# Second block's pooled products on 64 rows of the array each, alternating between two PSUM tiles

## The chip, the core and the metric

The kernel runs on one core of one Trainium2 chip. The metric is the device time of one execution in microseconds. TensorE multiplies, VectorE and ScalarE do elementwise work, SyncE's queue (SP) loads the weights. A matmul of TensorE takes its weights from SBUF by a load of its own and writes its sums into PSUM; the array has 128 rows, one for each partition over which a product is summed.

## What is computed

A program of four layers on 512 tokens of width 1024: two layers of a first block, then two of a second block. In each layer of the second block, one projection gives attention operands, a short convolution's operands, a pooling operand and three gates. The change is in the pooling branch:

```python
def pooling_mixer(u, w_grp, scale):
    # u: (B, S, 256); w_grp: (4, 64, 256)
    cs = jnp.cumsum(u, axis=1)
    for g, w in enumerate((2, 4, 8, 16)):
        csg = cs[:, :, 64 * g:64 * g + 64]
        lagged = jnp.pad(csg[:, :S - w], ((0, 0), (w, 0), (0, 0)))
        groups.append((csg - lagged) / counts - u[:, :, 64 * g:64 * g + 64])
    d = jnp.stack(groups, axis=2)
    out = jnp.einsum('bsgc,gcd->bsgd', d, w_grp).reshape(B, S, 1024)
    return out * scale

merged = g[:, :, 0] * y_attn + g[:, :, 1] * y_conv + g[:, :, 2] * y_pool
x = x + merged @ w_o[l]
```

Each of the four groups has 64 channels, so its product sums over 64 values and gives 256 output channels for each of the 512 tokens.

## The kernel before

Activations lie with channels on partitions and tokens along the free axis. Every product is made of three passes of rounded operands (`wH` by `hH`, `wH` by `hL`, `wL` by `hH`: high and low parts of weights and activations), each a matmul of 128 weights by 512 tokens.

Weights arrive in **units** of 128 x 2048. SP loads a unit into one of two `raw` buffers. ScalarE rounds it into `wH` (`split`, L1255), VectorE subtracts to get `wL` (`split`, L1688), and TensorE's `take_unit` waits for `wl_ready`, which that subtraction raises. `wH` and `wL` have two buffers, so ScalarE can round a unit only when TensorE has ended the unit before the previous one.

Results go through **jobs**. The PSUM tile `G` has four banks in two halves; `take_job` waits until the reader of the job before the last has freed its half (`job_free`), `end_job` raises `job_done` on the job's last matmul. VectorE's `step` waits for `job_done`, reads the half, frees it, and then, if told so, does the next unit's `split`. `psS` and `psT` are two further PSUM tiles of two banks, used by the attention before.

The order around the change, in each of the two layers: TensorE does the last two units of the pooling gate (`plain(h_op)`), then the pooled products, then the four gate units of the convolution. The first of these is called U+1 below, the second U+2. The pooled unit holds the weights of groups 0 and 2 on partitions 0 to 63 and of groups 1 and 3 on partitions 64 to 127; so do `PX_` and `PL`, the high and low parts of the pooled operand (`pd_op`, in the tile `wsr`). For each group there are two output tiles of 128 channels, `t` = 0 and 1, with three passes each: 24 matmuls per layer. The columns of a group's weights are zero in the other group's rows (the host writes only half of the rows), and each matmul runs over all 128 rows. Group 0 goes to a half of `G`, group 1 to `psS`, group 2 to `psT`, group 3 to the other half of `G`.

VectorE's program there is written out by hand: the last pooling gate is read (`scaled`, L1811), then `pools(0)` multiplies group 0 by its scale and gate (L2635, two instructions) and, as it is a `step`, splits U+1 (L1688); then `pools(1)` and `pools(2)` read `psS` and `psT` after `pooled_done`, and `pools(3)` is again a step, which splits U+2:

```python
step(lambda g: pools(0)(g).then_inc(job_free, 1))
for jj, bank in ((1, psS), (2, psT)):
    dve.wait_ge(pooled_done, (c.lay.v - 4) * 2 + jj)
    pools(jj)(bank)
step(lambda g: pools(3)(g).then_inc(job_free, 1))
```

Other lines that the prediction's steps touch: L1134, the attention scores, which are plain fp32 matmuls over 64 rows with the two heads of a pair in different halves of the rows; L949, scores of the first block over 128 rows; L552 transposes.

Of the kernel before, what the change touches and what calls it, by code (L numbers as in the profile page):

```python
# [22 lines left out]
P = 128  # L23
S = 512
M = 256
D = 1024
KT = D // P
# [102 lines left out]
class Pos:  # L130
# [5 lines left out]
    @property  # L136
    def v(self):
        return self.base + self.off
# [73 lines left out]
def program(nc, a, out, scratch):  # L212
    ctx = contextlib.ExitStack()
    with ctx:
# [8 lines left out]
        def sb(name, shape, dt=F32):  # L223
            return ctx.enter_context(nc.sbuf_tensor(name, shape, dt))

        def sem(name):
            return ctx.enter_context(nc.semaphore(name))
# [5 lines left out]
        wH = sb("wH", [P, 2, UNIT], F32R)  # L233
        wL = sb("wL", [P, 2, UNIT], F32R)
# [32 lines left out]
        G = ctx.enter_context(nc.psum_tensor("G", [P, 4, S], F32))  # L267
        psS = ctx.enter_context(nc.psum_tensor("psS", [P, 2, S], F32))
        psT = ctx.enter_context(nc.psum_tensor("psT", [P, 2, S], F32))
# [21 lines left out]
        def blocks(t, half):  # L291

            v = t.rearrange("p (n two l) -> p n two l", two=2, l=half)
            return v[:, :, 0, :], v[:, :, 1, :]
# [7 lines left out]
        for half in (8, 16, 32, 64, 128):  # L302
            n = S // half
# [61 lines left out]
        pooled_done = sem("pooled_done")  # L365
# [74 lines left out]
        def _(pe):  # L440
            c = Counts(pe)
# [5 lines left out]
            def take_job():  # L447

                pe.wait_ge(job_free, c.job.v + 1)

            def end_job(mm):
                mm.then_inc(job_done, 1)
                c.job.off += 1

            def passes(o, w0, w1, op, k, cols, first, last, swap=False, u=None):

                u = c.unit.p if u is None else u
                for n, (w, h) in enumerate(((wH, op[0]), (wH, op[1]), (wL, op[0]))):
                    wt, mv = w[:, u, w0:w1], h[:, k, cols]
                    mm = pe.matmul(o, mv if swap else wt, wt if swap else mv,  # L460
                                   start=first and n == 0, stop=last and n == 2)
                return mm
# [206 lines left out]
            pd_op = (wsr[:, PX_:PX_ + 2, :], wsr[:, PL:PL + 2, :])  # L669
# [45 lines left out]
            for l in range(2):  # L715
                if l == 0:
# [62 lines left out]
                    for n in range(2):  # L779
                        take_unit()  # L780
                        take_job()
                        for tt in range(ST):
                            for k in range(KT):
                                mm = passes(G[:, c.job.p * 2 + tt // 2, (tt % 2) * 256:(tt % 2) * 256 + 256],
                                            k * 256, k * 256 + 256, h_op, k, slice(tt * P, tt * P + P),
                                            k == 0, k == KT - 1, swap=True)
# [6 lines left out]
                    for lev in range(8):  # L793
                        for h in range(4):
                            n = lev * 4 + h
# [16 lines left out]
                            for o, ks, qs, w in parts:  # L812
                                q = q_[:, qs:qs + w]
                                if 0 < lev < 6:
                                    o, w, q = o // 2, w // 2, blocks(q, 2 ** (lev + 1))[1]
                                mm = pe.matmul(psS[:, n % 2, o:o + w], k_[:, ks:ks + P], q, start=True, stop=True)  # L816
                            mm.then_inc(hs_done, 1)

                            if h % 2 == 1:
                                k = n // 2 % KT  # L820
# [3 lines left out]
                                for t in range(2):  # L824
                                    w0 = k * 256 + t * P
                                    mm = passes(G[:, c.job.p * 2 + t, :], w0, w0 + P, h_op, k, slice(0, S),
                                                k == 0, k == KT - 1)
# [5 lines left out]
                    for h in range(4):  # L833
                        if h % 2 == 0:
                            take_job()
                        o = G[:, c.job.p * 2 + h % 2, :]
                        v = lambda tt: ws[:, GI + tt, h * P:h * P + P]

                        for ct in range(4):
                            pe.matmul(o[:, ct * P:ct * P + P], v(ct), ws[:, DD + h, ct * P:ct * P + P],  # L840
                                      start=(ct == 0), stop=False, skip_group_check=True)
                        for m in range(2):
                            pe.matmul(o[:, 256 * m + P:256 * m + 256], v(2 * m), hsx1[:, h, m, :],
                                      start=False, stop=False, skip_group_check=True)
                        for m in range(2):
                            mm = pe.matmul(o[:, 256:512], v(m), ws[:, SX2 + h, m * 256:m * 256 + 256],
                                           start=False, stop=(m == 1), skip_group_check=True)
# [32 lines left out]
                else:  # L880
# [73 lines left out]
                    for s_ in range(32 + PV_LAG):  # L954
# [6 lines left out]
                        if 0 <= r < 32:  # L961
# [3 lines left out]
                            for kt in range(r % ST + 1):  # L965
                                mm = pe.transpose(psT[:, r % 2, kt * P:kt * P + P],
                                                  ws[:, OP + r % 4, kt * P:kt * P + P], ident[:])
                            mm.then_inc(t_done, 1)
                        r = s_ - PV_LAG
                        if r >= 0:  # L970
                            h, qt = r // ST, r % ST
# [6 lines left out]
                            for kt in range(qt + 1):  # L978
                                mm = pe.matmul(G[:, 1 + 2 * (h % 2), qt * P:qt * P + P], ov[:, kt, h * P:h * P + P],
                                               opt[:, h % 2, kt, qt * P:qt * P + P], start=(kt == 0), stop=(kt == qt))  # L980
# [69 lines left out]
            for l in c.layers(2, **LAYER):  # L1050
# [5 lines left out]
                for k in range(KT):  # L1056
                    for n, (w, h) in enumerate(((fH, hH), (fH, hL), (fL, hH))):
                        mm = pe.matmul(G[:, c.job.p * 2, :], w[:, k * 8:k * 8 + P], h[:, k, :],  # L1058
                                       start=(k == 0 and n == 0), stop=(k == KT - 1 and n == 2))
# [3 lines left out]
                def token(tt, o):  # L1063
                    for k in range(KT):
                        mm = passes(o, k * 256, k * 256 + 256, h_op, k, slice(tt * P, tt * P + P),
                                    k == 0, k == KT - 1, swap=True)
                    return mm
# [3 lines left out]
                for tt in range(ST):  # L1071
                    mm = token(tt, G[:, c.job.p * 2 + tt // 2, (tt % 2) * 256:(tt % 2) * 256 + 256])
# [65 lines left out]
                def pv_pair(r):  # L1138
                    qt = fox_row(r)[1]
                    for kt in range(qt + 1):  # L1140
                        for h in (fox_row(r)[0], fox_row(r + 1)[0]):
                            lo = 64 * (h % 2)
                            mm = pe.matmul(G[lo:lo + 64, (h // 2) % 2 * 2 + 1, qt * P:qt * P + P],  # L1143
                                           ws[:, FV + kt, h * 64:h * 64 + 64], fpt[:, h % 2, kt, qt * P:qt * P + P],
                                           start=(kt == 0), stop=(kt == qt))
                    return mm
# [5 lines left out]
                for d in range(16 + 2):  # L1152
# [12 lines left out]
                    if 1 <= d <= 16:  # L1165
                        for r in (2 * d - 2, 2 * d - 1):
                            pe.wait_ge(p_ready, c.row.v + (r + 1))
                            wait(pe, pt_ready, c.row.v + (r - 1))
                            for kt in range(fox_row(r)[1] + 1):
                                mm = pe.transpose(psT[:, r % 2, kt * P:kt * P + P],  # L1170
                                                  ws[:, FP + r % 4, kt * P:kt * P + P], ident[:])
# [5 lines left out]
                    if r >= 0:  # L1177
# [9 lines left out]
                        mm = pv_pair(r)  # L1187
# [10 lines left out]

                take_unit()
                pe.wait_ge(pdl_ready, c.lay.v - 3)  # L1200
                for jj, bank in enumerate((None, psS, psT, None)):
                    if bank is None:
                        take_job()
                    for t in range(2):
                        o = 2 * jj + t
                        dst = G[:, c.job.p * 2 + t, :] if bank is None else bank[:, t, :]
                        mm = passes(dst, (KT + o) * P, (KT + o + 1) * P, pd_op, o // 4, slice(0, S), True, True)
                    if bank is None:
                        end_job(mm)
                    else:  # L1210
                        mm.then_inc(pooled_done, 1)
                c.unit.off += 1

                for n in range(4):
# [1659 lines left out]
```

## Time and profile before

| | us |
|---|---|
| three runs, median (lowest to highest) | 3120.57 (3120.07 to 3120.65) |
| span of the profiled execution | 3119.4 |
| TensorE busy with matmuls | 3097.3 (99%) |
| VectorE busy | 1563.7 (50%) |
| ScalarE busy | 1063.2 (34%) |
| TensorE's share of the chain that ended last | 91% |

The span runs from the first to the last instruction of one profiled execution; a run's time holds some 1.2 us more. "Busy" of TensorE counts a matmul from its issue to its end, and matmuls are pipelined, so starts are what to compare. The chain that ended last is followed back from the last instruction, at each step to what released it.

### The profile page before, as it was taken

How to read it: one execution, taken by the hardware profiler on the slowest of the kernel's cores; microseconds unless marked ns; L12 is line 12 of the kernel's file. 1: busy time of each engine (PE TensorE's matmuls, PEld its weight loads, DVE VectorE, ACT ScalarE, POOL GpSimd, SP SyncE). 2: the span in 40 equal slices, each digit the busy share in tenths (PEclk: the TensorE clock that was granted, in tenths of full speed). 3: DMA queues.
4: the chain of work that ended last, by engine and by line, in shares of the span. 5: the costliest groups of instructions: out<-in, count | busy, mean ns of one | idle time of the engine just before them, and what ended most of it. 6: DMA issues, size and time to landing. Idle time of an engine off the chain costs nothing.

```text
span 3119.4 us, 37101 instructions
## 1 busy us (share of the span) xinstructions
PE 3097.3 (99%) x15540; PEld 2594.3 (83%) x15540; DVE 1563.7 (50%) x1889; ACT 1063.2 (34%) x1155; POOL 237.6 (8%) x139
## 2 busy tenths in 40 slices
PE   9999999999999999999999999999999999999999
PEld 7798988888889798888888778888888878888887
DVE  7564555554335554555435764544433766444432
ACT  3223343443223433444323332333323332333321
POOL 0002100010000020010000000111000000100100
PEclk9999999999999999999999999999999999999999
DMA  4412412223321131222233122222232322222222
GB/s 170 115 55 73 144 55 90 99 94 108 120 97 68 48 142 55 85 99 99 95 108 116 58 92 101 90 99 93 103 108 89 95 82 95 95 95 96 94 106 95
DMA packets 47567, 297.72 MB, mean 95 GB/s; under 512 B 7075, under 2 KB 7331, under 8 KB 13396
## 3 DMA queue, kind: packets, MB, share of 16 engines
q1 hardware_dynamic: 42336, 285.91, 25.9%
q10 hardware_dynamic: 5108, 10.02, 1.4%
q8 instruction: 96, 1.57, 0.2%
q14 instruction: 27, 0.22, 0.0%
HBM read 291.16 MB, written 4.75 MB: 95 GB/s over the span
## 4 chain that ended last, share of the span: by engine, by line
PE 91%; DVE 5%; ACT 2%; issue 1%; DMA 0%; ACTq 0%; POOL 0%; DVEq 0%; SPq 0%
PE G L460 83%; DVE wL L1688 1%; ACT wH L1255 1%; PE psS L816 1%; DVE mxt L1920 1%; PE psS L520 1%; PE psS L1017 1%; PE psS L1134 0%; PE G L1143 0%; PE G L1024 0%; PE psT L552 0%; DVE ws L2477 0%; PE psT L1170 0%; PE G L1058 0%; PE psS L949 0%
## 5 line engine op out<-in xcount | busy, mean ns | idle before, releaser
L460 PE MATMUL G<-hH,wH 128*128 128x512 f32 x2560 | 1015.4, 397 | 9.1 <-DVE wL L1688 3.9
L460 PE MATMUL G<-hH,wL 128*128 128x512 f32 x2560 | 998.8, 390 | 0.0
L460 PE MATMUL G<-hL,wH 128*128 128x512 f32 x2560 | 997.7, 390 | 0.0
L1688 DVE TENSOR_TENSOR wL<-raw,wH 128x2048 fp32r<-128x2048 f32 x260 | 626.5, 2410 | 634.3 <-ACT wH L1255 634.0
L460 PE MATMUL G<-wsr,wH 128*128 128x512 f32 (+1 forms) x2512 | 745.9, 380 | 0.4
L1255 ACT ACTIVATE wH<-raw 128x2048 fp32r<-128x2048 f32 x263 | 501.7, 1908 | 591.7 <-PE G L460 573.1
L460 PEld LDWEIGHTS G<-hH,wH 128*128 128x128 f32 x2560 | 481.5, 188 | 124.1 <-issue 20.3
L460 PEld LDWEIGHTS G<-hH,wL 128*128 128x128 f32 x2560 | 481.0, 188 | 102.3
L460 PEld LDWEIGHTS G<-hL,wH 128*128 128x128 f32 x2560 | 481.9, 188 | 97.9 <-issue 1.2
L460 PEld LDWEIGHTS G<-wsr,wH 128*128 128x128 f32 x2512 | 464.3, 189 | 91.0 <-issue 1.5
L460 PE MATMUL G<-wsr,wL 128*128 128x512 f32 (+1 forms) x1256 | 476.1, 379 | 0.0
L460 PEld LDWEIGHTS G<-wsr,wL 128*128 128x128 f32 x1256 | 236.9, 189 | 44.5
L2725 POOL TENSOR_TENSOR wsr<-sq,wsr 128x1024 f32 x44 | 105.9, 2406 | 841.0 <-ACT wsr L1377 841.0
L1377 ACT ACTIVATE wsr<-sq 128x1024 f32 x44 | 46.7, 1061 | 231.7 <-DVE sq L1943 231.7
L2703 POOL TENSOR_TENSOR rsb<-ms,neghalf 128x4 f32<-128x4 f32 (+4 forms) x21 | 37.5, 1788 | 1116.7 <-DVE ms L1742 956.0
L1346 ACT ACTIVATE ws<-ws,mxt 128x128 f32<-128x128 f32 (+3 forms) x96 | 54.0, 563 | 193.9 <-DVE mxt L1920 193.3
L1863 DVE TENSOR_TENSOR x<-x,G 128x1024 f32<-128x1024 f32 x38 | 46.4, 1221 | 146.0 <-PE G L460 146.0
L460 PE MATMUL G<-wH,hH 128*128 128x256 f32 x384 | 112.1, 292 | 0.0
L460 PE MATMUL G<-wL,hH 128*128 128x256 f32 x384 | 108.6, 283 | 0.0
L460 PE MATMUL G<-wH,hL 128*128 128x256 f32 x384 | 108.5, 283 | 0.0
L1811 DVE TENSOR_TENSOR sq<-G,hmask 128x1024 f32<-128x1024 f32 x44 | 53.8, 1222 | 90.6 <-PE G L460 90.3
L1811 DVE TENSOR_TENSOR tn<-G,hmask 128x1024 f32<-128x1024 f32 x44 | 53.9, 1225 | 86.3 <-PE G L460 85.9
(291 smaller groups left out, 2510.3 us busy)
## 6 DMA issues: line engine op xcount, KB each, us to landing
raw<-in_units SPq DMA_DIRECT2D x263, 1024.0 KB, 4.8
ws<-bias_rows SPq DMA_DIRECT2D x2, 1536.0 KB, 14.7
bias_rows<-ws ACTq DMA_DIRECT2D x1, 2560.0 KB
x<-in_x SPq DMA_DIRECT2D x4, 512.0 KB, 7.5
ws<-in_mem ACTq DMA_DIRECT2D x2, 1024.0 KB, 4.7
ws<-bias_rows ACTq DMA_DIRECT2D x1, 2048.0 KB, 8.2
out_x<-x SPq DMA_DIRECT2D x3, 512.0 KB, 7.1
ws<-in_decay ACTq DMA_DIRECT2D x1, 1280.0 KB, 7.6
```

What stands on the lines that cost most here:

```text
L460: mm = pe.matmul(o, mv if swap else wt, wt if swap else mv, start=first and n == 0, stop=last and n == 2)
L520: mm = pe.matmul(st[:, col:col + 1], lhs, ones[:, 0:1], start=True, stop=True)
L816: mm = pe.matmul(psS[:, n % 2, o:o + w], k_[:, ks:ks + P], q, start=True, stop=True)
L1017: mm = pe.matmul(psS[:, r % 2, 0:M], ws[:, XQ + 2 * h + t, qt * P:qt * P + P], kx[:, 2 * h + t, :], start=(t == 0), stop=(t == 1))
L1255: activation(wH[:, g.p, :], raw[:, g.p, :], ACT.Copy).then_inc(wh_ready, 1)
L1346: return activation(p_, p_, ACT.Exp, bias=mxt[:, r % 4:r % 4 + 1], accum_out=den[:, r % 4:r % 4 + 1])
L1377: activation(aH[:, bass.ds(i * 2, 2), :], sq[:, 1], ACT.Copy).then_inc(ffn_h, 1)
L1688: V.tensor_tensor(wL[:, g.p, :], raw[:, g.p, :], wH[:, g.p, :].bitcast(F32), ALU.subtract)\
L1811: V.tensor_tensor(dst, g, rb_pair, ALU.mult).then_inc(job_free, 1)
L1863: V.tensor_tensor(x[:, 2 * jj:2 * jj + 2, :], x[:, 2 * jj:2 * jj + 2, :], g, ALU.add)\
L2703: W.tensor_tensor(dst[:, at:at + cols], ms[:, at:at + cols], neghalf[:].to_broadcast([P, cols]), ALU.pow)\
L2725: W.tensor_tensor(aL[:, bass.ds(i * 2, 2), :], sq[:, 1], aH[:, bass.ds(i * 2, 2), :].bitcast(F32), ALU.subtract).then_inc(ffn_ready, 1)
```

## The change

The matmuls of the pooled products are issued by a new function, `pooled_two`. Each takes 64 rows of weights and operand in place of 128. The two groups that share a column range of `pd_op` go in one run of twelve matmuls, alternating between partitions 0 to 63 and 64 to 127, and between two PSUM tiles. The weights, the three passes and their order within a group stay.

```diff
-                for jj, bank in enumerate((None, psS, psT, None)):
-                    if bank is None:
-                        take_job()
+                def pooled_two(k, first, second):
+                    u, done = c.unit.p, []
                     for t in range(2):
-                        o = 2 * jj + t
-                        dst = G[:, c.job.p * 2 + t, :] if bank is None else bank[:, t, :]
-                        mm = passes(dst, (KT + o) * P, (KT + o + 1) * P, pd_op, o // 4, slice(0, S), True, True)
-                    if bank is None:
-                        end_job(mm)
-                    else:
-                        mm.then_inc(pooled_done, 1)
+                        for n, (w, h) in enumerate(((wH, pd_op[0]), (wH, pd_op[1]), (wL, pd_op[0]))):
+                            for g, bank in enumerate((first, second)):
+                                rows, w0 = slice(64 * g, 64 * g + 64), (KT + 2 * (2 * k + g) + t) * P
+                                mm = pe.matmul(bank[:, t, :], w[rows, u, w0:w0 + P], h[rows, k, :],
+                                               start=n == 0, stop=n == 2)
+                                if n == 2 and t == 1:
+                                    done.append(mm)
+                    return done
+
+                take_job()
+                mm0, mm1 = pooled_two(0, G[:, c.job.p * 2:c.job.p * 2 + 2, :], psS)
+                end_job(mm0)
+                mm1.then_inc(pooled_done, 1)
+                take_job()
+                mm2, mm3 = pooled_two(1, psT, G[:, c.job.p * 2:c.job.p * 2 + 2, :])
+                mm2.then_inc(pooled_done, 1)
+                end_job(mm3)
                 c.unit.off += 1
```

On TensorE, the first half of the pooled products of a layer, before (each row a matmul, its line, its PSUM tile, its operands and its shape; `wsr` is the pooled operand):

```order
-L460 MATMUL G<-wsr,wH 128x512 [waits job_free,pdl_ready,wl_ready]
-L460 MATMUL G<-wsr,wH 128x512
-L460 MATMUL G<-wsr,wL 128x512
-L460 MATMUL G<-wsr,wH 128x512 x2
-L460 MATMUL G<-wsr,wL 128x512
-L460 MATMUL psS<-wsr,wH 128x512 x2
-L460 MATMUL psS<-wsr,wL 128x512
-L460 MATMUL psS<-wsr,wH 128x512 x2
-L460 MATMUL psS<-wsr,wL 128x512
```

The same place on TensorE in the changed kernel:

```order
+L1209 MATMUL G<-wsr,wH 128x512 [waits job_free,pdl_ready,wl_ready]
+L1209 MATMUL psS<-wsr,wH 128x512
+L1209 MATMUL G<-wsr,wH 128x512
+L1209 MATMUL psS<-wsr,wH 128x512
+L1209 MATMUL G<-wsr,wL 128x512
+L1209 MATMUL psS<-wsr,wL 128x512
+L1209 MATMUL G<-wsr,wH 128x512
+L1209 MATMUL psS<-wsr,wH 128x512
+L1209 MATMUL G<-wsr,wH 128x512
+L1209 MATMUL psS<-wsr,wH 128x512
+L1209 MATMUL G<-wsr,wL 128x512
+L1209 MATMUL psS<-wsr,wL 128x512
```

The matmuls into `G` and `psS` stood in two runs of six and now alternate, so the last one of group 0 is the 11th of the layer, where it was the 6th; the second take of a job (the next wait for `job_free`) stands before the 13th, where it stood before the 19th. Behind the 24th follows, in both kernels, the first matmul of U+1:

```order
 L460 MATMUL G<-hH,wH 128x512 [waits job_free,wl_ready]
```

On VectorE, which waits for group 0 and for which TensorE waits at U+1, the rows of the changed kernel from the last pooling gate to the split of U+2 (lines are 11 higher than before):

```order
L1822 TENSOR_TENSOR ws<-G,hmask 128x1024 [waits job_done]
L2646 SCALAR_TENSOR_TENSOR ws<-G,pc,ws 128x512 [waits act_read,job_done]
L2646 SCALAR_TENSOR_TENSOR ws<-G,pc,ws 128x512
L1699 TENSOR_TENSOR wL<-raw,wH 128x2048 [waits wh_ready]
L2646 SCALAR_TENSOR_TENSOR ws<-psS,pc,ws 128x512 [waits act_read,pooled_done]
L2646 SCALAR_TENSOR_TENSOR ws<-psS,pc,ws 128x512
L2646 SCALAR_TENSOR_TENSOR ws<-psT,pc,ws 128x512 [waits act_read,pooled_done]
L2646 SCALAR_TENSOR_TENSOR ws<-psT,pc,ws 128x512
L2646 SCALAR_TENSOR_TENSOR ws<-G,pc,ws 128x512 [waits act_read,job_done]
L2646 SCALAR_TENSOR_TENSOR ws<-G,pc,ws 128x512
L1699 TENSOR_TENSOR wL<-raw,wH 128x2048 [waits wh_ready]
```

Nothing moved on VectorE: the same instructions stand in the same order with the same waits.

## Rows read from the trace of the kernel before

**Rows 1.** The page: the span, and the chain's shares by engine.
```profile
span 3119.4 us, 37101 instructions
...
PE 91%; DVE 5%; ACT 2%; issue 1%; DMA 0%; ACTq 0%; POOL 0%; DVEq 0%; SPq 0%
```

**Rows 2.** Windows over both layers' pooled products: busy per engine (x instructions), clock, DMA.
```profile
1849.37:1854.81 5.44, 5.44 (x25) 4.50 (x24) 5.11 (x5) 2.86 (x2) 0.00 (x0) 1.00 0.00 0
2586.50:2591.95 5.45, 5.45 (x26) 4.51 (x25) 5.11 (x5) 2.86 (x2) 0.00 (x0) 1.00 0.01 2
```

**Rows 3.** Timeline, first layer: start us, duration us, engine, line, operation, out<-in.
```profile
1849.37 0.62 PE L460 MATMUL G<-wsr,wH 128*128 128x512 f32 x2
1849.57 1.22 DVE L1811 TENSOR_TENSOR ws<-G,hmask 128x1024 f32<-128x1024 f32 x1 [4.19 <-PE G L460]
...
1850.50 0.39 PE L460 MATMUL G<-wsr,wL 128*128 128x512 f32 x1
...
1850.93 1.41 DVE L2635 SCALAR_TENSOR_TENSOR ws<-G,pc,ws 128x512 f32<-128x512 f32 x2
...
1852.25 2.28 DVE L1688 TENSOR_TENSOR wL<-raw,wH 128x2048 fp32r<-128x2048 f32 x1
...
1854.45 1.41 DVE L2635 SCALAR_TENSOR_TENSOR ws<-psS,pc,ws 128x512 f32<-128x512 f32 x2
...
1854.59 0.19 PEld L460 LDWEIGHTS G<-hH,wH 128*128 128x128 f32 x1
...
1854.81 0.40 PE L460 MATMUL G<-hH,wH 128*128 128x512 f32 x1
...
1855.05 0.40 PE L460 MATMUL G<-hL,wH 128*128 128x512 f32 x1
...
1858.40 2.28 DVE L1688 TENSOR_TENSOR wL<-raw,wH 128x2048 fp32r<-128x2048 f32 x1
```

**Rows 4.** Timeline, second layer: the same split and the first matmul behind it.
```profile
2589.39 2.28 DVE L1688 TENSOR_TENSOR wL<-raw,wH 128x2048 fp32r<-128x2048 f32 x1
...
2591.95 0.40 PE L460 MATMUL G<-hH,wH 128*128 128x512 f32 x1
```

**Rows 5.** Timeline, TensorE: scores over 64 rows, scores over 128, each with its successor.
```profile
1773.65 1.13 PE L1134 MATMUL psS<-ws 64*128 64x512 f32 x4
1774.71 0.50 PE L460 MATMUL G<-hH,wH 128*128 128x512 f32 x1
...
1042.20 1.02 PE L949 MATMUL psS<-ws 128*128 128x512 f32 x2
1043.06 0.27 PE L966 MATMUL psT<-ident,ws 128*128 128x128 f32 x1
```

**Rows 6.** Timeline, TensorE: four transposes, followed by 64-row scores, then by a full matmul.
```profile
1686.05 0.60 PE L552 MATMUL psT<-ident,wide 128*128 128x128 f32 x4
...
1686.58 0.49 PE L1134 MATMUL psS<-ws 64*128 64x128 f32 x4
...
501.54 0.60 PE L552 MATMUL psT<-ident,wide 128*128 128x128 f32 x4
501.89 0.48 PE L460 MATMUL G<-hH,wH 128*128 128x512 f32 x1
```

**Rows 7.** Timeline: a wait of TensorE for a split elsewhere (first block).
```profile
509.12 2.29 DVE L1688 TENSOR_TENSOR wL<-raw,wH 128x2048 fp32r<-128x2048 f32 x1 [4.80 <-ACT wH L1255]
...
511.56 0.49 PE L460 MATMUL G<-hH,wH 128*128 128x512 f32 x1 [1.23 <-DVE wL L1688]
511.89 0.39 PE L460 MATMUL G<-hL,wH 128*128 128x512 f32 x1
```

**Rows 8.** Windows, TensorE alone: stretch, its length, busy (x instructions), granted clock, DMA.
```profile
7.50:12.00 4.50, 2.02 (x10) 1.00 1.04 427
...
1044.00:1047.00 3.00, 1.31 (x11) 1.00 0.00 0
1047.40:1050.70 3.30, 3.30 (x12) 0.53 0.00 0
```

## The prediction

> **What bounds the kernel now.** I read the page's chain first: TensorE carries 91% of the chain that ended last in a span of 3119.4 us [rows 1]. So at most places a matmul saved is time saved, but the share is an average over the whole program; what this change is worth is read at its own two places, one in each layer of the second block. The windows over the pooled products show them: 5.44 us in the first layer and 5.45 us in the second, TensorE busy all through, clock 1.00 [rows 2]. The timeline gives the pace: the 24 matmuls run one after another, 5.44 / 24 = 0.227 us from start to start, each record lasting 0.39 us because they are pipelined [rows 2, 3].
>
> The next thing to read is what stands behind the products. The following unit of weights, a gate unit I call U+1, may be multiplied only when VectorE has finished the low part of its split (L1688, `wL`). In the first layer that split starts at 1852.25 and ends at 1852.25 + 2.28 = 1854.53; TensorE loads the first weights of U+1 at 1854.59 and starts the matmul at 1854.81 [rows 3]. In the second layer the split ends at 2589.39 + 2.28 = 2591.67 and the matmul starts at 2591.95 [rows 4]. The split thus ends 0.28 us before a matmul that is itself not late. Today no wait shows because the pooled products last just as long as the VectorE chain beside them. **That near-tie decides the case.**
>
> The VectorE chain runs in program order: the last gate's read (1849.57 + 1.22 = 1850.79), the two multiplications of pooled group 0 (from 1850.93), then the split (from 1852.25) [rows 3]. VectorE was free at 1850.79, and the multiplication came 0.04 us after the sixth pooled matmul ended (1850.50 + 0.39 = 1850.89) [rows 3]. So the end of group 0's sixth matmul sets the end of the split.
>
> **What the change removes.** Still 24 matmuls of 512 columns per layer, but 12 pairs on different halves of the array's rows. Whether such pairs run beside each other, this trace shows on the attention scores: four 64-row matmuls of 512 columns (two scores, one in each half) take 1773.65 to 1774.71, 1.06 us, where two 128-row ones (one score) take 1042.20 to 1043.06, 0.86 us, 0.43 us each [rows 5]. One after another, four would need 4 x 0.43 = 1.72 us. So the halves do overlap, with some 1.06 - 0.86 = 0.20 us over one score's time. For the pooled products I take one pair at the price of one matmul now: 12 x 0.227 = 2.72 us, 2.72 us less per layer, 5.4 us in all before costs. The operands of the scores are plain fp32, those of the pooled products are rounded; no row has 64-row matmuls of the latter kind, so the pair is bounded by 0.213 us (the 0.43 us of a score's 512 columns halved) and 2 x 0.227 us.
>
> **What it adds on TensorE.** Entering the 64-row form: from four transposes to a score it takes 1686.05 to 1686.58, 0.53 us, and from four such transposes to a full matmul 501.54 to 501.89, 0.35 us [rows 6]; 0.18 us more. I bound the entry by 0 and 0.18 us and take 0.18, the only row that shows it. Leaving it costs up to the 0.20 us above, but there TensorE will be waiting anyway, so I put it at nothing; its cover is the wait worked out below, about 2 us.
>
> **What it moves.** Group 0 was six matmuls alone; now its sixth stands 11th in a row of 12 that mixes groups 0 and 1, in the sixth pair. With pairs at 0.227 us the sixth pair starts when the sixth matmul started before, plus the entry: VectorE's multiplication of group 0 starts 0.18 us later (1851.11), and the split of U+1 ends 0.18 us later, at 1854.71. The split's order on VectorE does not change, and it cannot move up: VectorE is free only at 1850.79, so the most to be had is 0.14 us, and that only if pairs were faster than single matmuls (6 x 0.014 = 0.08 us of that). The second take of a G half moves up from the 19th matmul to the 13th, to 1849.37 + 0.18 + 6 x 0.227 = 1850.91; it asks for the last gate's read, which ends at 1850.79 [rows 3], and a small wait there would be covered too.
>
> **Where TensorE stalls.** The last pair starts at 1849.37 + 0.18 + 11 x 0.227 = 1852.05 and ends 0.39 us later at 1852.44. Then its queue stops at the first matmul of U+1, which asks for `wL`; all of TensorE's program is queued behind it. It resumes as it did after another wait for a split: there the split ended at 509.12 + 2.29 = 511.41, the first matmul came at 511.56 and the second at 511.89, 0.33 us on instead of 0.227 [rows 7]. Here: 1854.71 + 0.15 + 0.33 = 1855.19 for the second matmul of U+1, against 1855.05 now [rows 3]: 0.14 us later. With the other ends (no entry cost, 0.06 us to the load as at 1854.59, pairs 0.08 us faster over six) it is 1854.53 - 0.08 + 0.06 + 0.33 = 1854.84, 0.21 us earlier. Per layer -0.2 to +0.14, for two layers -0.4 to +0.3 us. I take +0.3, whose terms are measured rows.
>
> **What else shifts and why it is free.** ScalarE's rounding of U+2 may start some 2.4 us earlier, as the unit buffer of the pooled weights comes free earlier; VectorE's part of that split starts at 1858.40 behind the four groups' multiplications, as before, and ends near 1860.8 [rows 3], while TensorE asks for it 48 matmuls after 1854.8, at 1854.8 + 48 x 0.227 = 1865.7. So the gain does not come back there. Groups 1 to 3 finish earlier, but VectorE takes them only after the split of U+1, now at 1854.45 [rows 3]. The 2.7 us per layer turn into a wait of 1854.86 - 1852.44 = 2.4 us.
>
> **The sum.** Profiled span 3119.4 us; the runs' median is 3120.57, so 1.2 us lie around the span, and I leave them. 3120.57 + 2 x 0.14 = 3120.85, given as 3120.8 us.
>
> **Rivals.**
> (1) *The pairs do not overlap, or only partly.* Then group 0's sixth matmul is the 11th in a plain row: 5 x 0.227 = 1.13 us later, plus 0.18 for the entry and 0.10 for the restart or the exit, and the split moves with it: +1.4 us per layer, 3120.57 + 2.8 = 3123.4. If a pair lasts as long as one matmul's record, 0.39 us, it is 5 x 0.163 = 0.8 us later, with the same additions +1.1 us per layer: 3122.8. Against it: 1.06 us for four in rows 5; for it: the weights of the pooled products change with every matmul.
> The Trainium skill ("TensorE: Matmul & The Clock Gate", section "The mechanism") says that a weight load overlaps matmuls in flight only when it goes to another row group; by that each pair would wait for the one before, as in the 0.39 us case. The trace speaks against it as a general rule: in the 5.44 us of the pooled products weight loads are busy for 4.50 us and matmuls for all 5.44, each of them on the full array [rows 2].
> (2) *The clock falls in the new wait.* A gap of 2.4 us in each layer stands between dense matmuls. For it: with 1.31 us of TensorE work in 3.0 us from 1044.0 on, the granted clock went from 1.00 (2.4 GHz) to 0.5 (1.2 GHz), 0.53 on average over the next 3.3 us [rows 8]. Against it: a gap of 2.48 us, with 2.02 us of TensorE work in the 4.5 us from 7.5 on, kept 1.00 [rows 8]. The price is half of 3.3 us, 1.65 us a time: 3122.5 for one fall, 3124.1 for two.
> (3) *Slower in earnest: every change between the halves empties the array.* Then each of the 24 matmuls takes its record's 0.39 us: 24 x 0.39 = 9.36 against 5.44, +3.9 us per layer, 3128.4. It would count as slower from 5.44 + 3.1 = 8.5 us, that is 0.357 us per matmul. Against it: rows 5, where matmuls in the two halves overlap.
> The Trainium skill ("TensorEngine Tiling (Array Packing)", section "Key Properties") says that changing the tiling mode drains the engine and changing the tile alone does not; by this there are two drains per layer, not 24, and rival 3 falls.
> (4) *The gain arrives.* If `wL` of U+1 were ready when the products end, 2 x (2.72 - 0.18 - 0.2) = 4.7 us come off: 3115.9. That needs the split some 2 us earlier, and rows 3 show VectorE working without a break from 1850.93 to its end.
> (5) *The change does not do what it says:* the two halves' matmuls come one by one in the queue. That is rival 1's time.
>
> **How the numbers follow.** Forecast 0.68; rival 1 (with 5) 0.13; rival 2 0.12; rival 3 0.03; rival 4 0.03; else 0.01. The forecast's own bounds, 3120.2 to 3120.9, widened by the 0.5 us that the three runs differ, are 3119.7 to 3121.4. To hold 8 in 10 the range reaches over rival 1 and over the clock falling up to twice: 3119.8 to 3124.2. About 0.2%, 6.2 us, is what a measurement of this kernel can tell from no change. Rival 4 and all of rivals 1 and 2 stay inside it, so faster 0.01, within 0.95, slower 0.04.
>
> **What would show it.** In the profile after: the pooled matmuls begin in pairs and the last begins near 1852.1 in the first layer; TensorE then has an idle stretch of about 2.4 us, once per layer, ended by VectorE's `wL`; the split of U+1 starts within 0.2 us of its old place; VectorE's multiplication of group 0 waits for TensorE and the ones of groups 1 to 3 for nothing. Wrong would be: no such wait (rival 4), the multiplication of group 0 starting over 0.8 us later (rival 1), or a granted clock of 0.5 behind the gap (rival 2).

## The result

The changed kernel takes 3125.07 us (median of 21 runs) where the kernel before, run between them, took 3120.66 us: ratio 1.0013, 95% interval [1.0007, 1.0018], so 2.2 to 5.6 us slower. Of the 21 runs one took 6822.83 us and is left out of the ratio and of the mean clocks below, as are one run of 5512.15 us and one of 3426.18 us in the experiments below; the other twenty lie between 3121.10 and 3128.02 us, median 3124.81. The time lies above the range of the prediction. The difference is under the 0.2% named there, but larger than chance.

The page of the changed kernel, span and chain by engine, beside [rows 1]:

```profile
span 3124.6 us, 37101 instructions
...
PE 91%; DVE 5%; ACT 2%; issue 1%; DMA 0%; ACTq 0%; POOL 0%; DVEq 0%; SPq 0%
```

The shares by engine are those of before to the percent; a change of 5 us in 3120 can't be read there. It is read at its two places. The timeline of the first layer, beside [rows 3] (start us, duration us, engine, line, operation, and in brackets the idle time ahead and its releaser):

```profile
1849.62 0.49 PE L1209 MATMUL G<-wsr,wH 64*128 64x512 f32 x1
...
1849.63 0.49 PE L1209 MATMUL psS<-wsr,wH 64*128 64x512 f32 x1
...
1849.73 1.23 DVE L1822 TENSOR_TENSOR ws<-G,hmask 128x1024 f32<-128x1024 f32 x1 [4.19 <-PE G L460]
...
1849.96 0.39 PE L1209 MATMUL G<-wsr,wH 64*128 64x512 f32 x1
1849.96 0.18 PEld L1209 LDWEIGHTS G<-wsr,wL 64*128 64x128 f32 x1
1849.96 0.39 PE L1209 MATMUL psS<-wsr,wH 64*128 64x512 f32 x1
1850.19 0.39 PE L1209 MATMUL G<-wsr,wL 64*128 64x512 f32 x1
...
1851.32 1.41 DVE L2646 SCALAR_TENSOR_TENSOR ws<-G,pc,ws 128x512 f32<-128x512 f32 x2 [0.36 <-PE G L1209]
...
1852.27 0.39 PE L1209 MATMUL psT<-wsr,wL 64*128 64x512 f32 x1
1852.28 0.39 PE L1209 MATMUL G<-wsr,wL 64*128 64x512 f32 x1
1852.64 2.29 DVE L1699 TENSOR_TENSOR wL<-raw,wH 128x2048 fp32r<-128x2048 f32 x1
...
1854.98 0.50 PE L460 MATMUL G<-hH,wH 128*128 128x512 f32 x1 [2.31 <-DVE wL L1699]
...
1855.32 0.53 PE L460 MATMUL G<-hL,wH 128*128 128x512 f32 x1
...
1855.65 0.63 PE L460 MATMUL G<-hH,wL 128*128 128x512 f32 x1
```

The last matmul of the pooled products of before, for the same count:

```profile
1854.58 0.40 PE L460 MATMUL G<-wsr,wL 128*128 128x512 f32 x1
```

Read it in four steps. The pairs run side by side: `G` and `psS` start 0.01 us apart, the second pair starts 0.33 us after the first and each later one 0.23 us after the one ahead of it, and from the first start to the last end the 24 matmuls take 1852.28 + 0.39 - 1849.62 = 3.05 us, where before they took 1854.58 + 0.40 - 1849.37 = 5.61 us (the 5.44 us of [rows 2] run to the start of the next matmul). The VectorE chain is no shorter: the multiplication of group 0 and the split stand 0.39 us behind their places of [rows 3], 0.16 us of which was there already at the last gate's read (1849.73 against 1849.57). So TensorE waits 2.31 us for `wL`. And behind the wait the matmuls slow down: the third starts 0.33 us behind the second and lasts 0.63 us, where a record lasted 0.40.

The windows of TensorE alone (stretch, length, busy with instructions, granted clock, DMA share, GB/s) show the pooled products, the wait and the stretch behind it; the last three rows are the wait and the stretch behind it in the second layer, and one more stretch, in the attention of the second layer:

```profile
1849.60:1852.70 3.10, 3.07 (x25) 1.00 0.00 0
1852.70:1854.98 2.28, 0.00 (x0) 1.00 0.01 4
1855.30:1858.60 3.30, 3.30 (x9) 0.52 0.67 251
2593.14:2595.45 2.31, 0.01 (x1) 1.00 0.00 0
2596.00:2599.30 3.30, 3.30 (x9) 0.52 0.78 281
2449.00:2453.00 4.00, 4.00 (x13) 0.57 0.73 262
```

The same stretches behind the pooled products in the kernel before:

```profile
1855.10:1858.40 3.30, 3.30 (x16) 1.00 0.76 273
2592.20:2595.50 3.30, 3.30 (x16) 1.00 0.73 253
```

In both layers the granted clock went from 1.00 (2.4 GHz) to 0.5 (1.2 GHz) within 0.6 us behind the wait, and nine matmuls ran where sixteen had. What that costs is read at a later row that both traces have, here VectorE's next read of a gate, first of before, then of after:

```profile
1876.80 1.22 DVE L1811 TENSOR_TENSOR ws<-G,hmask 128x1024 f32<-128x1024 f32 x1 [4.21 <-PE G L460]
```

```profile
1878.68 1.23 DVE L1822 TENSOR_TENSOR ws<-G,hmask 128x1024 f32<-128x1024 f32 x1 [5.71 <-PE G L460]
```

The two are 1.88 us apart, against 0.16 us ahead of the pooled products: the first place cost 1.72 us. Of that 0.11 us is the restart (second matmul of U+1 at 1855.32 - 0.16 against 1855.05 [rows 3]) and 1.61 us the clock. The last matmul ahead of the second place, first of before, then of after:

```profile
2586.27 0.39 PE L460 MATMUL G<-hH,wL 128*128 128x512 f32 x1
```

```profile
2589.78 0.39 PE L460 MATMUL G<-hH,wL 128*128 128x512 f32 x1
```

There the traces are 3.51 us apart, 1.6 us of which came at the fall at 2449; at the end they are 3124.6 - 3119.4 = 5.2 us apart, so the second place cost 1.7 us. The change itself thus accounts for 3.4 us of the 5.2 in this pair of executions. The fall at 2449 stands far from any changed row, none of the other eight profiled executions has it, and nothing here ties it to the change. The clock also falls in the first block, in every profiled execution, of the kernel before too: there near 259, 282, 1047 and 1068 us. Where these falls lie and how long they last differs from execution to execution.

### The profile page after: what moved, and what is told of

Read it like the earlier page. It is cut to its first block, busy times and chain, and to the rows that moved or that the text cites. A ratio compares the mean times of both kernels' runs of the same rounds, so it can differ in the third digit from the quotient of the medians.

```text
span 3124.6 us, 37101 instructions
## 1 busy us (share of the span) xinstructions
PE 3097.6 (99%) x15540; PEld 2592.1 (83%) x15540; DVE 1563.7 (50%) x1889; ACT 1063.4 (34%) x1155; POOL 237.6 (8%) x139
## 3 DMA queue, kind: packets, MB, share of 16 engines
q8 instruction: 96, 1.57, 0.2%
## 4 chain that ended last, share of the span: by engine, by line
PE 91%; DVE 5%; ACT 2%; issue 1%; DMA 0%; ACTq 0%; POOL 0%; DVEq 0%; SPq 0%
PE G L460 83%; DVE wL L1699 1%; ACT wH L1266 1%; PE psS L816 1%; DVE mxt L1931 1%; PE psS L520 1%; PE psS L1017 1%; PE psS L1134 0%; PE G L1143 0%; PE G L1024 0%; PE psT L552 0%; DVE ws L2488 0%; PE psT L1170 0%; PE psS L949 0%; PE G L1058 0%
```

## The experiments

Each kernel was run in five rounds beside the kernel before, the first four in one series (before: 3121.37 us), the last three in another (before: 3121.15 us). The windows come from one profiled execution of each, with two places in it; each run besides has a mean granted clock, read to 0.001.

**Filling the wait.** The second twelve pooled matmuls are issued three times over into the same tiles, so that TensorE has work until the split is done; the repeated products replace themselves.

```
                 take_job()
+                pooled_two(1, psT, G[:, c.job.p * 2:c.job.p * 2 + 2, :])
+                pooled_two(1, psT, G[:, c.job.p * 2:c.job.p * 2 + 2, :])
                 mm2, mm3 = pooled_two(1, psT, G[:, c.job.p * 2:c.job.p * 2 + 2, :])
```

> The changed kernel, with the twelve matmuls of groups 2 and 3 issued three times over in each layer (each repetition starts its sums anew, so the last one counts). This fills TensorE's wait behind the pooled products with 64-row pairs, 2 x 6 x 0.233 = 2.8 us against a wait of 2.31 us. Theory G (the 2.3 us without matmuls let the clock fall to 0.5 for 3.3 us, 1.7 us per layer): no fall behind the pooled products, TensorE ends them 0.3 to 0.5 us later than the split, time 3120.7 + 2 x 0.4 = 3121.5 us. Rival H (64-row matmuls use half of the array and by that let the clock fall, gap or no gap): a fall in each layer stays or gets longer, 3125 us or more.

Measured: 3121.49 us, ratio 1.0001 [0.9992, 1.001]. (Its profiled execution is the slowest of its eleven, with a clock of 0.50 behind a gap of 3.18 us at the program's start; the median is what counts.) No wait for `wL` stood behind the pooled products, and the windows behind them kept the clock:

```profile
1858.00:1861.00 3.00, 3.00 (x20) 1.00 0.21 33
2596.00:2599.00 3.00, 3.00 (x20) 1.00 0.38 49
```

So 24 more matmuls per layer on the same TensorE gave back what the shorter stage had lost. The 64-row products as such cost nothing here; what they leave behind does.

**Filling a part of it.** Only three pairs are repeated.

```
-                def pooled_two(k, first, second):
+                def pooled_two(k, first, second, ts=(0, 1)):
...
-                    for t in range(2):
+                    for t in ts:
...
+                pooled_two(1, psT, G[:, c.job.p * 2:c.job.p * 2 + 2, :], (0,))
                 mm2, mm3 = pooled_two(1, psT, G[:, c.job.p * 2:c.job.p * 2 + 2, :])
```

> The changed kernel, with the three pairs of the first output tile of groups 2 and 3 issued once more in each layer: the wait behind the pooled products shrinks from 2.31 to about 1.6 us. Theory G: if the length of the wait decides, the clock falls less often or not at all, 3121.0 us without a fall and 3122.7 to 3124.4 with one or two. Rival H: 3125 us, as the changed kernel.

Measured: 3121.11 us, ratio 1.0001 [0.9992, 1.001]. The timeline of TensorE at both restarts, and the windows behind them:

```profile
1856.51 0.50 PE L460 MATMUL G<-hH,wH 128*128 128x512 f32 x1 [1.64 <-DVE wL L1700]
...
2593.74 0.50 PE L460 MATMUL G<-hH,wH 128*128 128x512 f32 x1 [1.64 <-DVE wL L1700]
```

```profile
1857.00:1860.00 3.00, 3.00 (x15) 1.00 0.72 246
2594.00:2597.00 3.00, 3.00 (x14) 1.00 0.64 210
```

A wait is still there, 1.64 us long instead of 2.31, and the clock stays. The wait alone, then, costs nothing (it takes the place of matmul time); the loss is what the clock does behind a longer one.

**The same gap without 64-row matmuls.** The kernel before with full-array products, but groups 1 to 3 without their two low-part passes, so TensorE has twelve matmuls instead of 24 and ends as early as in the changed kernel. Left out of the computation: those passes.

```
-                        mm = passes(dst, (KT + o) * P, (KT + o + 1) * P, pd_op, o // 4, slice(0, S), True, True)
+                        if jj == 0:
+                            mm = passes(dst, (KT + o) * P, (KT + o + 1) * P, pd_op, o // 4, slice(0, S), True, True)
+                        else:
+                            mm = pe.matmul(dst, wH[:, c.unit.p, (KT + o) * P:(KT + o + 1) * P], pd_op[0][:, o // 4, :],
+                                           start=True, stop=True)
```

> The kernel before, all matmuls on 128 rows, but groups 1, 2 and 3 get one pass in place of three (the two passes with low parts are left out there, so those products are less exact): 12 matmuls of 0.227 us in place of 24. Group 0 keeps its six and its place, so the split of the next unit keeps its time, and TensorE waits some 2.2 us for it, as in the changed kernel but without 64-row matmuls. Theory G: the clock falls in both layers as in the changed kernel, 3120.7 + 0.2 + 2 x 1.65 = 3124.2 us, and nothing is gained from 24 matmuls less. Rival H: no fall, 3120.9 us.

Measured: 3125.14 us, ratio 1.0014 [1.0005, 1.0023], as slow as the changed kernel with less work. Its restarts and the windows behind:

```profile
1855.43 0.50 PE L460 MATMUL G<-hH,wH 128*128 128x512 f32 x1 [2.34 <-DVE wL L1692]
...
2594.09 0.80 PE L460 MATMUL G<-hH,wH 128*128 128x512 f32 x1 [2.34 <-DVE wL L1692]
```

```profile
1856.00:1859.30 3.30, 3.30 (x11) 0.60 0.76 290
2594.10:2597.40 3.30, 3.30 (x8) 0.50 0.71 206
```

A wait of 2.34 us, and the clock falls at both places, with no 64-row product in the kernel. This separates the two explanations: the wait brings the fall, not the form of the matmuls.

**Not alternating.** The changed kernel with the same 64-row matmuls, same tiles and same number, but all six of one group queued ahead of the six of the other.

```
-                    for t in range(2):
+                    for gg, t in ((0, 0), (0, 1), (1, 0), (1, 1)):
...
-                            for g, bank in enumerate((first, second)):
+                            for g, bank in ((gg, (first, second)[gg]),):
```

> The 64-row matmuls of the changed kernel in the order of the groups (six of group 0, six of group 1, and so on) and not alternating, in the same PSUM tiles. Theory: in one half of the rows they go one after another, 24 x 0.227 us = 5.4 us and no wait behind them; 0.3 us of entry and exit per layer; 3121.3 us, no fall. If the halves' matmuls overlapped whatever their order, or if 64-row matmuls alone brought the clock down (rival H): 3124 to 3125 us.

Measured: 3123.78 us, ratio 1.001 [1.0001, 1.0019]. The expectation missed. TensorE's timeline in the first layer:

```profile
1849.15 0.73 PE L1209 MATMUL G<-wsr,wH 64*128 64x512 f32 x2
1849.72 0.39 PE L1209 MATMUL G<-wsr,wL 64*128 64x512 f32 x1
1849.73 0.49 PE L1209 MATMUL psS<-wsr,wH 64*128 64x512 f32 x1
1849.96 0.39 PE L1209 MATMUL G<-wsr,wH 64*128 64x512 f32 x1
1850.07 0.39 PE L1209 MATMUL psS<-wsr,wH 64*128 64x512 f32 x1
...
1850.42 0.39 PE L1209 MATMUL G<-wsr,wL 64*128 64x512 f32 x1
...
1852.37 0.39 PE L1209 MATMUL G<-wsr,wL 64*128 64x512 f32 x1
...
1854.51 0.50 PE L460 MATMUL G<-hH,wH 128*128 128x512 f32 x1 [1.76 <-DVE wL L1699]
```

The matmuls of `psS` begin while three of the six of `G`, queued ahead of them, have not begun: the two row halves run as two streams, each 0.23 us apart, the second some 0.6 us behind the first. The 24 take 1852.37 + 0.39 - 1849.15 = 3.61 us, not 5.61. So the overlap comes from the row halves; the alternation only takes off the last 0.56 us. The Trainium skill ("TensorE: Matmul & The Clock Gate", section "The mechanism") has matmuls start strictly in program order; these rows differ. And since the products are short here too, a wait stands behind them, 1.76 us in both layers, with these windows behind it in the first and the second:

```profile
1855.50:1858.90 3.40, 3.40 (x9) 0.51 0.94 308
2594.00:2597.00 3.00, 3.00 (x15) 1.00 0.76 268
```

One fall of two, which fits a loss between that of the changed kernel and none.

**Making the work behind it ready earlier.** VectorE's split of U+1 is done in two instructions of 1024 columns, and TensorE starts on the first when it is done; it asks for the second ahead of its fifth row tile (a row tile is 128 of the rows over which a product is summed).

```
-                step(lambda g: pools(0)(g).then_inc(job_free, 1))
+                step(lambda g: pools(0)(g).then_inc(job_free, 1), unit=False)
+                dve.wait_ge(wh_ready, c.unit.v + 1)
+                for at, done in ((slice(0, 1024), wl_half), (slice(1024, UNIT), wl_ready)):
+                    V.tensor_tensor(wL[:, c.unit.p, at], raw[:, c.unit.p, at], wH[:, c.unit.p, at].bitcast(F32),
+                                    ALU.subtract).then_inc(done, 1)
+                c.unit.off += 1
...
+                def low_half(k):
+                    if k == 4:
+                        take_unit()
...
+                pe.wait_ge(wl_half, c.lay.v - 3)
+                take_job()
+                end_job(two_tiles(h_op, range(KT), operand=low_half))
```

> The changed kernel, with VectorE's part of the split behind the pooled products done in two halves: TensorE starts that unit when the first 1024 columns are ready and asks for the rest before its fifth k. The first half takes some 1.15 us where the whole took 2.28, so TensorE resumes 1.1 us earlier and waits 1.2 us in place of 2.31. Theory G: after a wait that short the clock stays at 1.00 and the earlier restart is kept, 3120.7 + 0.3 - 2 x 1.1 = 3118.8 us. If the clock falls after this wait too: 3120.5 to 3122.1 us. If something else than the split holds TensorE (a PSUM half, a transfer): no change against the changed kernel, 3125 us.

Measured: 3118.37 us, ratio 0.999 [0.9981, 0.9999]: faster than before by 0.3 to 5.9 us. (The changed kernel was not run in this series; its fastest run, 3121.10 us, is slower than the slowest here, 3120.41 us.) VectorE's split, TensorE's restarts and the windows behind them:

```profile
1853.63 2.35 DVE L2663 TENSOR_TENSOR wL<-raw,wH 128x1024 fp32r<-128x1024 f32 x2
```

```profile
1854.90 0.50 PE L460 MATMUL G<-hH,wH 128*128 128x512 f32 x1 [1.24 <-DVE wL L2663]
...
2591.10 0.50 PE L460 MATMUL G<-hH,wH 128*128 128x512 f32 x1 [1.24 <-DVE wL L2663]
```

```profile
1855.00:1858.30 3.30, 3.30 (x15) 1.00 0.29 62
2591.20:2594.50 3.30, 3.30 (x15) 1.00 0.34 70
```

The two halves cost 2.35 us of VectorE instead of 2.29; TensorE waits 1.24 us instead of 2.31, and the clock stays.

**In four pieces.** The same with four instructions of 512 columns, and TensorE's waits for the later three ahead of its third, fifth and seventh row tile. The edit of VectorE's part, against the kernel with two halves:

```
-                for at, done in ((slice(0, 1024), wl_half), (slice(1024, UNIT), wl_ready)):
+                for at, done in [(slice(512 * q, 512 * q + 512), wl_half if q < 3 else wl_ready) for q in range(4)]:
```

> As the kernel with the split in two halves, but in four quarters of 512 columns. TensorE resumes when the first quarter is ready, 0.6 us after the split starts: a wait of about 0.8 us. Theory G: 3120.7 + 0.3 - 2 x 1.6 = 3117.8 us, no fall. If each piece costs VectorE a fixed price or TensorE runs into the later quarters: 3118.8 us or more.

Measured: 3119.26 us, ratio 0.9992 [0.9983, 1.0001]. The wait is shorter again, and the clock 1.00 behind both:

```profile
1854.46 0.50 PE L460 MATMUL G<-hH,wH 128*128 128x512 f32 x1 [0.71 <-DVE wL L2665]
...
2590.10 0.50 PE L460 MATMUL G<-hH,wH 128*128 128x512 f32 x1 [0.71 <-DVE wL L2665]
```

0.53 us less waiting per layer should be 1.1 us less in all, and at the first place the profiled executions show it. VectorE's next read of a gate, first with two halves, then with four pieces:

```profile
1877.00 1.22 DVE L1831 TENSOR_TENSOR ws<-G,hmask 128x1024 f32<-128x1024 f32 x1 [2.97 <-PE G L460]
```

```profile
1876.56 1.23 DVE L1833 TENSOR_TENSOR ws<-G,hmask 128x1024 f32<-128x1024 f32 x1 [2.29 <-PE G L460]
```

The read ahead of the pooled products started at 1850.72 and 1850.82, so the stage takes 26.28 us with two halves and 25.74 with four pieces, against 27.23 before and 28.95 in the changed kernel. In the runs' times the gain does not show: 3119.26 us is more than the 3117.8 expected, and the intervals of two halves and four pieces overlap nearly whole. The profiled execution of the four pieces lost clock elsewhere, behind a gap at the program's start that the edit does not touch:

```profile
9.72 0.50 PE L460 MATMUL G<-hH,wH 128*128 128x512 f32 x1 [1.79 <-DVE wL L2052]
```

```profile
9.75:13.05 3.30, 3.30 (x9) 0.59 1.05 436
```

So whether four pieces beat two over many runs is not settled.

**The halves without the change.** The edit of the two halves, on the kernel before.

> The kernel before with the split in two halves and its pooled products untouched: TensorE is busy with them to 0.28 us behind the whole split, so the halves have nothing to give. 3120.7 us, within 0.5 us. Rival: if the halves gain by themselves (another stall of the kernel that they remove), 3119 us or less, and the gain of the two kernels above isn't the pooled products'.

Measured: 3120.81 us, ratio 0.9999 [0.999, 1.0008], with no wait behind the pooled products. Splitting early is worth nothing where TensorE is not waiting; the gain of the two-halves kernel is the pooled products' own, let through.

The waits and the clock behind them in the profiled executions, and the mean granted clock over the runs:

| kernel | wait for `wL` behind the pooled products, us | falls at the two places | mean granted clock (runs) |
|---|---|---|---|
| before | none | 0 | 0.9974 (34), 0.9974 (27) |
| changed kernel | 2.31, 2.31 | 2 | 0.9960 (20) |
| same gap, 128 rows | 2.34, 2.34 | 2 | 0.9959 (11) |
| not alternating | 1.76, 1.76 | 1 | 0.9963 (11) |
| filled in part | 1.64, 1.64 | 0 | 0.9975 (11) |
| filled | none | 0 | 0.9975 (11) |
| split in two | 1.24, 1.24 | 0 | 0.9975 (11) |
| split in four | 0.71, 0.71 | 0 | 0.9972 (11) |

The last column says for all the runs what the falls say for one execution of each: the three kernels that are slower than before are the three at 0.9963 and under. As an estimate from it, with the changed kernel's runs from another series than those of before, 0.9974 - 0.9960 of 3120 us is 4.4 us of matmul time, about the whole of the loss.

The length of a gap alone does not tell whether the clock falls behind it. At the program's start TensorE waits in every profiled execution; there the clock stayed at 1.00 behind gaps of 1.57, 1.75, 1.75, 2.12, 2.48, 2.58 and 2.64 us and fell behind 1.79 and 3.18. Behind a gap of 1.43 us in the first block's attention (near 1031 us in before, 1032 in the changed kernel), between matmuls with smaller pauses, it fell in two of the nine executions. And the clock fell with no gap ahead: in the kernel before, near 282 and 1068 us, at the end of 32 matmuls of one column (L511) that kept TensorE busy for 3.77 and 4.03 us.

## Why the prediction was wrong

**What held.** The bound: the near-tie of TensorE's products and VectorE's split decides the case, and the whole gain became a wait: 2.31 us, where 2.4 was worked out. The pair's price: 0.23 us a pair, where 0.227 was taken. The shift of the split: 1852.64 - 0.16 against 1852.25, so 0.23 us, where 0.18 was taken: the first pair came 0.31 us behind the last full matmul and the second 0.33 us behind the first, where the pace is 0.227, so these two steps make 0.19 us, and the pairs' slower pace most of the rest. The restart: +0.11 us, where +0.14 was taken; the matmul came 0.05 us after the split's end instead of 0.15. Together these steps give 3120.57 + 2 x 0.11 = 3120.8, the forecast's own figure.

**What failed** is the step from the wait to the time: the sum 3120.57 + 2 x 0.14 lets TensorE resume at full clock, so the fall of the clock stands in it with nothing, where the two falls cost 1.6 us each. It was left to rival 2, whose mechanism and price were on paper: 1.65 us a fall, 3124.1 for two, against 1.61 us measured at the first place. But it got a chance of 0.12, because one row of the kernel before kept 1.00 through a gap of 2.48 us [rows 8]. That row was too little to go by. It stands at 7.5 us, at the program's start, and is one execution: at the same place the clock fell in two of the nine executions profiled here, once behind a gap of only 1.79 us. The four gaps of 2.31 and 2.34 us profiled here, each between stretches of matmuls without a pause, all ended in a fall. With one row for and one against, and none of a gap of this length between such stretches, a chance near one half would have been fairer, and the price would have entered the likeliest time or at least the middle of the range. The range had its top at two falls exactly, with nothing added for what the runs of one kernel differ (3121.1 to 3128.0 here), so the median passed it by 0.9 us.

**The other rivals.** (1) fell: the pairs overlap. The Trainium skill's rule named there ("TensorE: Matmul & The Clock Gate", section "The mechanism"), that a weight load overlaps only matmuls of another row group, does not hold in these rows: at 1849.96 the load of the next weights of `G` starts together with a matmul of `G`, in the same half. (3) fell: no change between halves empties the array, 0.23 us a pair. (4) fell here, but came about in part as soon as half of `wL` was ready earlier: 1.24 us of wait remain, and 3118.37 us is the time then. (5) fell in an unforeseen way: even one group after the other, the halves overlap.

**What stays open.** What, beside its length, decides whether a gap ends in a fall is not shown: a wait of 1.76 us did in one layer and not in the other, and at other places 1.43 and 1.79 us did where 2.64 us did not. Nor is it shown why the clock also fell at 2449 us in the changed kernel's profile, or, with 4.4 us between the medians (4.2 by the twenty runs) against 3.4 us accounted for in the trace, whether more than these two places is lost on average; the interval, 2.2 to 5.6 us, holds both.

## What to carry to other kernels

A TensorE stage that is just covered by the preparation of the next weights can't be made shorter alone: what is saved becomes a wait, so shorten the preparation, or hand it over in pieces, in the same change. Then price the new wait as a possible fall of the clock, by rows of a similar wait between similar matmuls, from more than one execution, and don't let one row from another place stand for it. To see which of the two costs the time, fill the gap with repeated work: if the time goes back while the work grows, it was the clock.

## What the runs showed of the hardware

Matmuls of 64 rows in different halves of the array run side by side even when the queue holds all of one half's ahead of the other's: 24 of them in 3.61 us, against 3.05 us alternating and 5.61 us on the full array. Each half keeps the pace of a full matmul, 0.23 us for 512 columns.

A wait of TensorE of 2.31 to 2.34 us between matmuls without a pause, behind the pooled products, ended four times out of four in a stretch of about 3.3 us at a granted clock of 0.5 to 0.6, worth 1.6 us; one of 1.76 us once in two, one of 0.71 to 1.64 us never in six. These are counts at one place, not a limit: elsewhere the clock fell behind 1.43 and 1.79 us and stayed behind 2.64 us.
